# Strassen's scheme for 16 of the 22 depth tiles of four feed-forward down products

## The reference, cut to what matters

```
D_MODEL = 1024; SEQ = 512; DEPTH = 2; D_FF = 2816

def swiglu(x, w_gu, w_down):
    gate, up = jnp.split(x @ w_gu, 2, axis=-1)
    return (jax.nn.silu(gate) * up) @ w_down

def hybrid_layer(x, mem_n, ...):
    h = layer_norm(DEEPNORM_ALPHA * x + 0.5 * swiglu(x, ffn1_w_gu, ffn1_w_down), ln_g[0], ln_b[0])
    ...
    h = layer_norm(DEEPNORM_ALPHA * h + merged @ w_out, ln_g[1], ln_b[1])
    return layer_norm(DEEPNORM_ALPHA * h + 0.5 * swiglu(h, ffn2_w_gu, ffn2_w_down), ln_g[2], ln_b[2])
```

## Time and profile before

| | us |
|---|---|
| median of 3 runs | 3560.33 (3557.63 to 3562.96) |
| profiled execution, its own time | 3558.9 |
| its span | 3557.1 |
| PE busy | 3502.0 (98%) |
| DVE busy | 2226.9 (63%) |
| ACT busy | 1679.6 (47%) |
| mean granted TensorE clock | 0.995 |

### The profile page before, as it was taken

One profiled execution on the slowest core, in us unless ns is written; L12 is line 12 of the kernel. 1 busy time (PEld: TensorE's weight loads), 2 busy tenths in 40 slices (PEclk: granted clock), 3 DMA queues, 4 the chain that ended last, 5 costly groups with the idle time before them and its releaser, 6 DMA issues.

```text
span 3557.1 us, 49763 instructions
## 1 busy us (share of the span) xinstructions
PE 3502.0 (98%) x19256; PEld 2932.2 (82%) x19256; DVE 2226.9 (63%) x4229; ACT 1679.6 (47%) x3243; POOL 111.3 (3%) x132
## 2 busy tenths in 40 slices
PE   9999999999999999999999999999999999999999
PEld 7898878877888987998888877888977677788887
DVE  5566656556775667566665566765676786666643
ACT  5354455554353545454555543553455443444432
POOL 0010000000000100010000000001000000000000
PEclk9999999999999999999999999999999999999999
DMA  5474331112335743574221112255522222233332
GB/s 154 131 175 143 116 95 48 45 47 72 90 105 138 173 122 98 140 172 125 83 66 47 47 60 91 93 134 151 152 79 86 69 66 84 77 94 93 95 95 86
DMA packets 198276, 358.86 MB, mean 101 GB/s; under 512 B 22102, under 2 KB 26359, under 8 KB 198040
## 3 DMA queue, kind: packets, MB, share of 16 engines
q1 hardware_dynamic: 178840, 321.32, 29.8%
q0 software_dynamic: 18432, 33.56, 5.6%
q10 hardware_dynamic: 768, 0.79, 0.1%
HBM read 350.60 MB, written 4.72 MB: 100 GB/s over the span
## 4 chain that ended last, share of the span: by engine, by line
PE 93%; DVE 4%; ACT 2%; issue 1%; DMA 0%; DVEq 0%; ACTq 0%
PE bank L2490 21%; PE bank L2499 21%; PE bank L2491 21%; PE bank L2525 6%; PE bank L2527 6%; PE bank L2528 6%; PE bank L2478 2%; PE bank L2473 1%; PE bank L2568 1%; PE bank L2661 1%; PE bank L2671 1%; PE bank L2536 1%; PE bank L2759 1%; PE bank L2588 1%; DVE w_lo L3235 0%
## 5 line engine op out<-in xcount | busy, mean ns | idle before, releaser
L2490 PE MATMUL bank<-page_r,w_hi 128*128 128x512 f32 (+1 forms) x3446 | 1383.4, 401 | 21.9 <-DVE w_lo L3235 14.7
L2499 PE MATMUL bank<-page_r,w_lo 128*128 128x512 f32 (+1 forms) x3446 | 1359.7, 395 | 0.0
L2491 PE MATMUL bank<-page_r,w_hi 128*128 128x512 f32 (+1 forms) x3446 | 1349.8, 392 | 0.0
L2490 PEld LDWEIGHTS bank<-page_r,w_hi 128*128 128x128 f32 x3446 | 650.0, 189 | 182.5 <-DVE w_lo L3235 18.8
L2813 ACT ACTIVATE w_hi<-raw 128x512 fp32r<-128x512 f32 x864 | 532.8, 626 | 558.3 <-PE bank L2499 550.1
L2499 PEld LDWEIGHTS bank<-page_r,w_lo 128*128 128x128 f32 x3446 | 649.2, 188 | 145.7
L2491 PEld LDWEIGHTS bank<-page_r,w_hi 128*128 128x128 f32 x3446 | 649.9, 189 | 141.6 <-issue 3.6
L3235 DVE TENSOR_TENSOR w_lo<-raw,w_hi 128x512 fp32r<-128x512 f32 x864 | 574.9, 686 | 150.2 <-ACT w_hi L2813 149.8
L2525 PE MATMUL bank<-page_r,w_hi 128*128 128x256 f32 x1792 | 503.7, 281 | 2.5 <-DVE w_lo L3253 2.5
L2528 PE MATMUL bank<-page_r,w_lo 128*128 128x256 f32 x1792 | 503.4, 281 | 0.0
L2527 PE MATMUL bank<-page_r,w_hi 128*128 128x256 f32 x1792 | 503.4, 281 | 0.0
(11 more groups left out here) (322 smaller groups left out, 3462.9 us busy)
## 6 DMA issues: line engine op xcount, KB each, us to landing
raw<-weights SPq DMA_DIRECT2D x864, 256.0 KB, 2.7
raw<-pairs SPq DMA_DIRECT2D x320, 256.0 KB, 3.3
raw<-pairs POOLq DMA_DIRECT2D x128, 256.0 KB, 5.8
page_f<-x_t SPq DMA_DIRECT2D x8, 256.0 KB, 5.2
bias_rows<-page_f SPq DMA_DIRECT2D x8, 256.0 KB, 2.0
page_f<-bias_rows SPq DMA_DIRECT2D x8, 256.0 KB, 3.9
out_t<-page_f SPq DMA_DIRECT2D x12, 128.0 KB, 1.8
cst<-consts SPq DMA_DIRECT2D x4, 272.0 KB, 3.5
```

The costliest lines, as they stand in the source:

```text
L2490: self.e.matmul(o, hi, X.hi[kt], start=first, stop=False)
L2491: self.e.matmul(o, hi, X.lo[kt], start=False, stop=False)
L2499: last = self.e.matmul(o, lo, X.hi[kt], start=False, stop=final)
```

## The change

16 of the 22 tiles of H are gathered in two groups of eight (`Group`), and their share of the down product is made by pairs too: `Added(m, m+1)` multiplies two output tiles by the eight tiles of a group, in 7 products of 4 pieces with 256 columns, and adds each product straight into the residual by DVE (`pair_add`, six instructions of 128 x 256). The 6 remaining tiles of H go through `update` as before, 6 blocks deep where they were 11. The 4 gate and up pairs that fill group one are followed by 2 more, then by its 4 `Added` pairs; the rest likewise (`BEHIND`). The sums of H that the scheme needs are made in "chores" (`tiles_of`): for two tiles of H, DVE makes four dependent sums of 128 x 256 and three rests of 128 x 512 and one of 128 x 256, ACT four roundings. They are slotted into the pairs, and the second group's wait until the first group's products are through (`may_begin`). `ffn_times` leaves the rounding and the rest of a plain tile to the chores. The memory keys and values of layer 1 are stored to DRAM after they are made and loaded again later, and `prepare_memory` is stepped six at a time. `NPAIR` goes from 64 to 96, `NSLAB` from 864 to 736.

```diff
-NSLAB = 1120 - 4 * 64
-NPAIR = 64
+NPAIR = 4 * (16 + 8)
+NSLAB = 1120 - 4 * NPAIR
-FIRST = 11
+GROUP = 8
+GROUPS = 2
+BEHIND = (2, 1)
...
-    def update(self, mat, H, scale, stats, tiles=8, k0=0, beside=None, begun=None):
+    def update(self, mat, H, scale, stats, tiles=8, k0=0, beside=None, begun=None, pace=3):
...
-                    self.bg.steps(3)
+                    self.bg.steps(pace)
...
+    def chore(self, n=1):
+        while n > 0 and self.chores and self.chores[0][0].may_begin():
+            if next(self.chores[0][1], self) is self:
+                self.chores.pop(0)
+            n -= 1
...
+        H = Operand(FT - GROUPS * GROUP)
+        gated = [Gated(self, up, j, X, groups[j // GROUP] if j < GROUPS * GROUP else H) for j in range(ALONE, FT)]
+        jobs, end = [], 0
+        for i, G in enumerate(groups):
+            begin, end = end, (i + 1) * GROUP + BEHIND[i] - ALONE
+            jobs += gated[begin:end]
+            jobs += [Added(self, down, m, G, scale, range(i * GROUP, (i + 1) * GROUP), m == DT - 2) for m in range(0, DT, 2)]
+        jobs += gated[end:]
...
-            self.ffn_act(k, gate, lift, s, h, l)
+            self.ffn_times(k, gate, lift, s)
...
-            H.join((h, l, k["rest"]))
-            self.pages.give(s, k["rest"])
+            groups[0].take(s, k["times"], 1.0)
...
+                    if self.next_block % 3 == 0 and groups[0].split < 2:
+                        self.chore()
...
-        self.paired(up, range(ALONE, FIRST), X, H, head, ahead(FIRST * DT), follow)
...
-        self.paired(up, range(FIRST, FT), X, H, head, ahead(NSLAB * SLAB), follow)
+        follow = Later(self.product(down, 0, H, k0=GROUPS * GROUP))
+        self.paired(jobs, ahead(NSLAB * SLAB), follow)
         self.drop(X, (self.lanes["pair"].tensor, self.lanes["pair"].raised[0]))
-        return self.update(down, H, scale, Spread(self, after, after.count == 2), k0=FIRST, beside=mem, begun=follow)
+        return self.update(down, H, scale, Spread(self, after, after.count == 2), k0=GROUPS * GROUP, beside=mem,
+                           begun=follow, pace=6)
...
+            if l:
+                self.set_aside(l)
+                yield
...
+            if l:
+                self.bring_back(l)
...
+    def pair_add(self, k, bank, m, half, scale, made, before):
+        x = self.R[m].f[:, half]
+        self.wait_ge(*made)
+        self.wait_ge(*before)
+        self.e.scalar_tensor_tensor(out=x, in0=bank.cols(256), scalar=scale, in1=x, op0=ALU.mult, op1=ALU.add) \
+            .then_inc(k.lane.vector, 1)
```

More of the change, by code:

```diff
@@ L983, in step, with paired @@
+    def paired(self, jobs, ahead, follow):
+        prev = None
+        for n in range(len(jobs) + 1):
+            cur, nxt, later = (jobs[n + i] if n + i < len(jobs) else None for i in range(3))
             def step(p):
@@ L985, in step, with last_one @@
                     p.step()
+            def last_one():
+                if cur and not nxt:
+                    next(ahead)
             if cur:
[L988 to L992, removed]
-            if prev:
[L994 to L998, removed]
-            if cur:
[L1000 to L1008, removed]
+                cur.open()
+                cur.product("q1", cur.a, True)
+            if prev:
+                prev.lifted()
+            if cur:
+                cur.step()
+                last_one()
+                cur.product("q5", cur.c, True)
+                cur.seed()
+                cur.step()
+            if n == 0:
                 step(nxt)
@@ L1014, in paired @@
             if prev:
-                self.pair_product(prev, "q4", prev.b, False, prev.k["c22"])
-            if cur and not nxt:
-                next(ahead)
+                prev.product("q4", prev.b, False, "lifted")
+            last_one()
             if cur:
[L1019 to L1022, removed]
+                cur.kept()
+                cur.step()
+                cur.product("q6", cur.b, False, "seed")
@@ L1023, in paired @@
             step(nxt)
             if prev:
-                prev.k.will(vector="h1")
-                self.pair_last(prev.k, prev.b, prev.s)
-                self.banks.give(prev.b, prev.k["h1"])
+                prev.last()
+            self.chore()
             if cur:
[L1029 to L1033, removed]
+                last_one()
+                cur.product("q3", cur.c, False, "kept")
+                cur.halfway()
@@ L1034, in paired @@
             if prev:
-                h, l = take(), take()
-                prev.k.will(scalar="round")
-                self.pair_round(prev.k, prev.s, h)
+                prev.rounded()
+            self.chore()
             step(nxt)
             if cur:
[L1040 to L1045, removed]
+                last_one()
+                cur.product("q2", cur.a, False, "seed")
+                cur.first()
@@ L1046, in paired @@
             step(nxt)
             if prev:
[L1048 to L1051, removed]
+                prev.rested()
+            self.chore()
             if cur:
[L1053 to L1056, removed]
+                cur.product("q7", cur.b, False, "halfway")
+                cur.gate()
@@ L2070, in step, with open, product, seed @@
             next(self.steps, None)
+    def open(self):
+        self.a, self.c = self.o.banks.take(), self.o.banks.take()
+    def product(self, name, bank, first, after=None):
+        o = self.o
+        hi, lo, ready = self.units.pop(name)
+        self.k.will(tensor=name)
+        o.pair_matmuls(self.k, bank, first, hi, lo, ready, [self.k[after]] if after else [], self.operands(name))
+        bank.covered = True
+        o.his.give(hi, self.k[name])
+        o.raws.give(lo, self.k[name])
+        o.bg.now += 1.42
+    def seed(self):
+        self.b = self.o.banks.take_covered()
+        self.k.will(scalar="seed")
+        self.o.pair_seed(self.k, self.a, self.b)
+class Gated(Pair):
+    def __init__(self, o, mat, j, X, H):
+        super().__init__(o, mat, j, FT + j, range(4), range(4, 8))
+        self.X, self.H = X, H
     def operands(self, name):
@@ new lines, in first, with gate, lifted @@
+    def first(self):
+        k = self.k.will(vector="c12")
+        self.o.pair_first(k, self.c, self.t, self.s)
+        self.o.banks.give(self.c, k["c12"])
+    def gate(self):
+        k = self.k.will(scalar="silu2 silu1")
+        self.o.pair_gate(k, self.a, self.s)
+        self.o.banks.give(self.a, k["silu1"])
+    def lifted(self):
+        k = self.k.will(vector="lifted h2")
+        self.o.pair_lift(k, self.b, self.t)
+        self.o.pair_join(k, self.t, self.s)
+        self.o.pages.give(self.t, k["h2"])
```

261 lines of the change are left out of this document (204 added, 57 removed).

## The result

The changed kernel takes 3565.77 us (median of 20 runs, 3559.75 to 3572.46) where the kernel before takes 3559.79 (20 runs): a ratio of 1.0019, 95% interval 1.0012 to 1.0025. It is slower by 0.19%: the interval leaves out 1, but the difference is just inside the 0.2% that the prediction takes for no change. The forecast was 3546, 0.4% faster. The profiled execution took 3565.72 us, its span is 3563.9, 6.8 us above that of before.

A forecast was written before the change was run, and what follows sets the result against it. The prediction took PE, busy 3502.0 of 3557.1 us, to bound the kernel. A gain of 40.4 us, less waits and clock losses, summed to -14.5 us against 3560.33, giving 3546 us, range 3526 to 3566.

The forecast's parts named there:

- PE's work, 32 pairs: Four FFNs: 32 pairs of 9.94 us each replace 16 down blocks of 11.2 us, taking 40.4 us off PE.
- pairs with chores: Pairs into which a chore falls: 0.45 us of PE waiting for each of 5 chores in four FFNs, +9.0 us.
- starts of the FFNs: Start of each FFN: rounding of finished tiles taken out of line saves 1.0 us in each of four, -4.0 us.
- last tile of H: First down blocks after the pairs: PE waits 1.15 us for the last tile's rest in each of four FFNs, +4.6 us.
- three tails, waiting: Last stretch of three FFNs: PE waits 3.5 us each for DVE's statistics ahead of the var matmul, +10.5 us.
- clock behind them: Behind the three tails: granted clock halves after PE's wait, 2.5 us a fall, half of three taken, +3.8 us.
- memory preparation: FFN1 of layer 0: preparation loses 40 blocks of cover and is stepped twice as fast, +2.0 us.
- My test of the gain: Whole kernel: if PE's busy time does not fall by 35 to 45 us, the price of a pair is wrong.
- Chores between pairs: DVE's chore work in pairs: 4.0 us against 3.0 idle, partly covered; 0.45 us for each of 5, four FFNs, +9.0.
- Rival C: Pairs' weights come late in 24 pairs in a row; 0.35 us a pair gives 3580 us; chance 0.14.
- Rival B: Tails wait 6.3 us each by full DVE durations, clock falls at all three, chores cost 0.8: 3565 us; chance 0.18.

The follow-up runs named there:

- eighth kernel: Changed kernel with lent unit, spread chores (first group's last too), later rests of weights, five ready blocks told first, no POOL sums: 3533.45 us, 0.9928 of kernel before.
- Experiment 2: Changed kernel with each chore's steps spread over two pairs, except a group's last chore: 3556.05 us, ratio 0.9989 to the kernel before.
- experiment 3: Changed kernel with rests of weights told one slab later from the last stretch's fifth output tile: 3558.61 us, ratio 0.9996 to the kernel before.
- experiment 1: Changed kernel with the lent raw unit used as the short-lived page, not for a tile of H: 3564.64 us, ratio 1.0010 to the kernel before.
- experiment 6: Changed kernel with lent unit, spread chores and later rests of weights, plus running sums behind the mean on POOL: 3550.78 us, 0.9977 of kernel before.

## Why the prediction was wrong

| step | forecast, us | measured, us |
|---|---|---|
| PE's work, 32 pairs | -40.4 | -40.4 |
| pairs with chores | +9.0 | +21.1: chores about 15, other slips about 6 |
| starts of the FFNs | -4.0 | about -3.4 |
| last tile of H | +4.6 | +5.7 |
| three tails, waiting | +10.5 | +10.1 (3.61, 3.62, 2.87) |
| clock behind them | +3.8 | about +6.2 (1.8, 2.4, 2.0) |
| memory preparation | +2.0 | about +4.1 |
| not in the sum | 0 | about +3.4 |

The measured column is worked out from the starts of PE's matmuls in the two traces: in pairs and waits by the spacing beyond 0.233 and 0.118 us, in the clock and the memory preparation by how far the same matmul falls behind that of the kernel before. Its last line is what is left of the span's 6.8 us. For the memory preparation: from the first matmul of FFN1's last pair to the same matmul behind its last stretch it is 139.55 us before and 117.09 now, 22.5 less where 28 us of blocks are gone, and 1.4 of the difference is the last tile. Four of the seven steps held within about a microsecond. The gain was there in full, by the spacing of the pairs without a chore. Of the 21.3 us between the sum of -14.5 and the 6.8, the pairs with chores are 12.1; the clock and the memory preparation are 2.4 and 2.1.

**My test of the gain was ill made.** A fall of PE's busy time outside 35 to 45 us was to show my price of a pair wrong. It fell by 20.6, yet pairs without a chore take the 9.94 us forecast. Busy time also counts part of every wait: before 1195.51 the next matmul is 0.46 late, of which 0.30 is shown as idle, and the 0.11 behind it is busy as well: 0.27 a wait, so 8 to 16 us for one or two waits in 29 pairs. With some 6 us at half clock, which count as busy too, that is 14 to 22 us, against 19.8 missing. The eighth kernel, with few of these waits and no half clock behind its tails, is at 32.9 below:

```profile
PE 3469.1 (98%) x20408; PEld 2965.1 (84%) x20408; DVE 2442.6 (69%) x4645; ACT 1754.1 (50%) x3339; POOL 167.2 (5%) x196
```

The spacing of the starts, not busy time, is what a price should be tested by.

**The step that failed first is "Chores between pairs".** It put 0.45 us on each of 5 chores. The trace has six to eight long pairs in each FFN, most at +0.72. The count was wrong: six of an FFN's eight chores fall into pairs, two of the first group's and four of the second's (two gate and up pairs fill group one and two more follow, where the section on the change says four and two). The price was wrong because I followed one chain only. I asked whether L3256 would be in time for the first product and found over a microsecond to spare, which held. I did not ask it of the next rest, L3253, which has a further rest of the chore ahead of it and only the spacing of one product after the first. And each wait costs 0.11 us more than its length. The 1.0 us too much that I worked out (4.0 of work, 3.0 of idle time) was right as an upper end; I took less than half of it, on the argument that the next pair would take up the backlog. It can't, because L3491 waits for PE in each pair, and so a backlog that delays PE in one pair is paid there. Experiment 2 shows that where the work was put, not its amount, was the price.

**The clock** was given half a chance at three tails. It fell at all three, for 1.8, 2.4 and 2.0 us, a little less than the 2.5 that I put on one fall. Rows 11 and 12 had given one case each way, and I split the difference; experiment 3 shows that at these tails the one long wait was the cause.

**Late data.** Rival C named the mechanism, with a `raw` unit that the groups hold now and then. The sum put it at nothing. It is one unit for some 16 of 24 pairs, and its price in the pairs is the 4.9 us that experiment 1 gave back (21.1 to 16.2), 3.7 of it in three slips of 0.9 to 1.7 us; the 0.15 us for every pair did not come. All but six of the pairs without a chore stayed at 9.94.

Rival B gave 3565, and 3565.77 was measured. It was right in two of its three parts (chores near the upper end, the clock at all three tails) and wrong in the third: the tails waited 3.6 us by DVE's spacing of 0.60, not 6.3 by full durations. That its number came out is luck: the 8.8 us too much for the tails stand against the late data, the memory preparation and the line that is not in the sum, which it did not have. The Trainium skill, "VectorE: DVE Perf Modes", section Terms, states that a flush stands behind every operation and that the next can't issue until the pipe is empty. Read as the forecast read it for the 6.3 us, as full durations one behind the other, the trace does not agree: independent instructions of the chore and the tail start 0.60 us apart and last 0.68. Whether a shorter flush lies within the 0.60 no run here shows.

**What stays open**: about 3.4 us outside the places that I priced. Of these, 1.1 are one more fall of the clock at 549 us, behind a wait that the change hardly touched (below), and 1.2 come between 2654 and 2820 us, where the stretches at half clock lie elsewhere than before. Why the clock falls at one such wait and not at another stays open, and so does why the memory preparation became dearer: 2.5 us of PE's waits there are for rests of the memory's norm (L3583), which the kernel before had in time.

## What to carry to other kernels

Work that is moved beside a saturated engine is priced by what stands behind it in its queue: follow every later instruction that the saturated engine waits for, not only the next one, up to the point where the queue itself waits for that engine. If the sum of work fits over two periods but not over one, cut it into steps small enough for each period, and tell blocks that are ready before the one that is not. An idle engine is no free place while it shares ports with the busy one.

## What the runs showed of the hardware

**The clock does not go by the length of one idle time alone.** In the kernel before a wait of 2.22 us at 549 left the clock at 1.00. In the changed kernel the same wait is shorter and halves it. Timeline of PE and the window at it:

```profile
549.81 0.79 PE L2665 MATMUL bank<-page_r,w_hi 128*128 128x512 f32 x1 [2.09 <-DVE w_lo L3424]
550.40 0.63 PE L2666 MATMUL bank<-page_r,w_hi 128*128 128x512 f32 x1
```

```profile
548.00:552.00 4.00, 2.19 (x5) 1.81 (x6) 3.75 (x9) 1.86 (x4) 0.00 (x0) 0.73 0.19 66
```

In experiment 6, which is alike there, the same wait is as long and leaves the clock at 1.00:

```profile
545.52 0.50 PE L2680 MATMUL bank<-page_r,w_hi 128*128 128x512 f32 x1 [2.08 <-DVE w_lo L3439]
```

```profile
545.00:549.00 4.00, 3.48 (x21) 3.07 (x22) 2.46 (x7) 0.57 (x2) 0.00 (x0) 1.00 0.08 30
549.00:553.00 4.00, 4.00 (x33) 3.77 (x32) 2.58 (x4) 1.13 (x3) 0.00 (x0) 1.00 0.24 65
```

So a wait near two microseconds may or may not cost 1.1 us more (the changed kernel's lag behind the kernel before grows from 1.16 to 2.27 us there), and the same program part can differ between two kernels that are alike there. The Trainium skill, "TensorE: Matmul & The Clock Gate", Part 1, says that an idle array falls back to 1.2 GHz; the tails agree, with 3.36 us of standing.

**A wait costs more than its length.** The first matmul behind one holds the next up for 0.23 us instead of 0.12 at 256 columns (1195.51 to 1195.74) and for 0.34 instead of 0.23 at 512 (1310.76 to 1311.10), at a granted clock of 1.00.
